# A hybrid encoder layer on one core: prompt attention with head pairs in TensorE row and column groups, expert gathers that skip empty places, gate and up weights in 8 KB pieces

## The reference

```python
h   = rmsnorm(x) * (1 + scale1) + shift1              # adaLN, modulation from silu(c) @ w_ada
q, k, v, cb, cc, cv, ga, gb = split(h @ w_in)         # 8 heads of 64
att = prompt_attention(q, k, v, rel_bias)             # per chunk of 64 frames: own + 8 previous chunks
                                                      # softmax(q k^T / 8 + bias(distance)) @ v
att_s = sample_attention(...)                         # 16 new frames against 512 cached keys + themselves
mix = (sigmoid(ga) * (att @ w_pa) + sigmoid(gb) * (short_conv(cb, cc, cv) @ w_pb)) @ w_o
x  += gate1 * mix
h2  = rmsnorm(x) * (1 + scale2) + shift2
# MoE: top-1 of 4 groups, then top-2 of its 8 experts; 32 experts, 1024 -> 512 -> 1024 (SwiGLU)
y   = sum over 2 experts of weight * (silu(h2 @ w_gate[e]) * (h2 @ w_up[e])) @ w_down[e]
x  += gate2 * y;  out = rmsnorm(x) * final_g
```

## Time and profile before

| | us |
|---|---|
| median of 3 runs | 1829.62 (1826.26 to 1830.77) |
| the profiled execution, its own time | 1827.22 |
| its span, first to last instruction | 1825.5 |
| PE busy | 1657.6 (91%) |
| DVE busy | 936.5 (51%) |
| ACT busy | 755.9 (41%) |
| POOL busy | 260.9 (14%) |
| mean granted TensorE clock | 0.959 of full |

### The profile page before, as it was taken

The page is one execution under the profiler, slowest core; times in us unless marked ns, Lnnn a source line. Parts: engine busy times, 40 slices in busy tenths (PEclk is TensorE's granted clock), DMA queues, the critical chain, the costliest instruction groups (busy, mean ns, idle before and its releaser), DMA issues.

```text
span 1825.5 us, 23013 instructions
## 1 busy us (share of the span) xinstructions
PE 1657.6 (91%) x8761; PEld 1380.1 (76%) x8761; DVE 936.5 (51%) x1108; ACT 755.9 (41%) x869; POOL 260.9 (14%) x327
## 2 busy tenths in 40 slices
PE   6994999999899999999998992499999999999977
PEld 1244997888599899999997882377787778777853
DVE  0450110555502552222224447488888888888857
ACT  0221221665311121112112222177777777777753
POOL 2003601110000000000000004112122121212003
PEclk9996999999999999999999996699999999999988
DMA  9857612000921111112126332399999999999967
GB/s 342 291 109 178 247 58 67 30 1 1 329 71 47 36 39 48 53 56 79 52 63 216 113 104 104 119 398 398 398 399 398 399 398 399 397 400 396 400 219 285
DMA packets 194748, 371.37 MB, mean 203 GB/s; under 512 B 10699, under 2 KB 69107, under 8 KB 194546
## 3 DMA queue, kind: packets, MB, share of 16 engines
q1 hardware_dynamic: 170784, 289.92, 43.9%
q0 software_dynamic: 18976, 62.93, 10.7%
q10 hardware_dynamic: 4914, 17.49, 2.4%
HBM read 324.49 MB, written 47.89 MB: 204 GB/s over the span
## 4 chain that ended last, share of the span: by engine, by line
PE 71%; DMA 13%; DVE 8%; issue 3%; ACT 3%; another core or an unknown queue 2%; SPq 0%; POOL 0%; DVEq 0%; ACTq 0%; PEldq 0%; POOLq 0%
PE ps L1547 13%; PE ps L1548 12%; PE ps L1549 12%; DMA mraw<-in_w_e_down_dram 10%; PE ps L1530 4%; PE ps L1876 4%; PE ps L1877 3%; PE ps L1883 3%; PE ps L1674 3%; PE ps L1655 2%; PE ps L1903 2%; PE ps L1911 2%; PE ps L1904 2%; ACT mhi L931 2%
## 5 line engine op out<-in xcount | busy, mean ns | idle before, releaser
L1064 DVE TENSOR_TENSOR mlo<-mraw,mhi 128x2048 fp32r<-128x2048 f32 x188 | 427.7, 2290 | 79.0 <-ACT mhi L931 78.8
L931 ACT CAST mhi<-mraw 128x2048 fp32r<-128x2048 f32 x192 | 366.8, 1914 | 113.5 <-DMA mraw<-in_w_e_down_dram 78.4
L1547 PE MATMUL ps<-hTh,ring_r 128*128 128x384 f32 x864 | 293.8, 340 | 34.6 <-DVE ring_r L1064 28.5
L1548 PE MATMUL ps<-hTl,ring_r 128*128 128x384 f32 x864 | 292.9, 339 | 0.0
L1549 PE MATMUL ps<-hTh,ring_r 128*128 128x384 f32 x864 | 292.6, 339 | 0.0
L1876 PE MATMUL ps<-mhi,xTh 128*128 128x512 f32 x512 | 204.7, 400 | 2.7 <-DVE xTl L1064 2.4
L1877 PE MATMUL ps<-mhi,xTl 128*128 128x512 f32 x512 | 201.3, 393 | 0.0
L1547 PEld LDWEIGHTS ps<-hTh,ring_r 128*128 128x128 f32 x864 | 165.5, 192 | 35.9 <-DVE ring_r L1064 26.7
L1064 DVE TENSOR_TENSOR ring_r<-ring_f,ring_r 128x1024 fp32r<-128x1024 f32 x56 | 68.3, 1224 | 198.5 <-ACT ring_r L741 198.1
L1549 PEld LDWEIGHTS ps<-hTh,ring_r 128*128 128x128 f32 x864 | 165.4, 191 | 0.0
L1548 PEld LDWEIGHTS ps<-hTl,ring_r 128*128 128x128 f32 x864 | 165.4, 191 | 0.0
(11 more groups left out here) (306 smaller groups left out, 2513.0 us busy)
## 6 DMA issues: line engine op xcount, KB each, us to landing
mraw<-in_w_e_gate_dram SPq DMA_DIRECT2D x64, 1024.0 KB
mraw<-in_w_e_up_dram SPq DMA_DIRECT2D x64, 1024.0 KB
mraw<-in_w_e_down_dram SPq DMA_DIRECT2D x64, 1024.0 KB, 12.6
aring<-in_w_ada_dram SPq DMA_DIRECT2D x24, 1024.0 KB
ring_f<-in_w_in_dram SPq DMA_DIRECT2D x80, 256.0 KB, 4.5
y_d<-yy ACTq DMA_DIRECT2D x32, 512.0 KB, 6.8
y_d<-zrow POOLq DMA_DIRECT2D x68, 128.0 KB, 4.0
kc<-in_cache_attn_k_dram SPq DMA_DIRECT2D x8, 1024.0 KB, 7.8
```

The lines of the kernel that those rows point to most:

```text
L931: nc.scalar.copy(mhi[j][:], mraw[j][:]).then_inc(s["gu_hi" if j < 4 else "d_hi"], 1)
L1064: V.tensor_tensor(out, value, high.bitcast(F32), ALU.subtract).then_inc(sig, 1)
L1547: mm(out, xh, wh, start=start, stop=False)
L1548: mm(out, xh, wl, start=False, stop=False)
```

## The change

Prompt attention: the scores of both heads of a pair are issued together, each with its own 64 partitions of `qT` and `kT` (row groups) and no `qz`. After the exponentials DVE computes the reciprocal of each unit's sum, and POOL multiplies the unit's probabilities by it in place. `S` gets four buffers, holds scores and probabilities, and `PT` gets three. The values of both heads are made together, `v` as the stationary operand with 64 columns, each head in its own column group, so the result comes out transposed as `qT` wants it; `att_t` and the multiplication on DVE go. PE order per pair p: scores(p+2), prob_t(2p), values(p-1), prob_t(2p+1).

Experts: empty places hold an index beyond the rows, and the gather skips these. The 1024 input features are numbered p*8+k instead of k*128+p for gate, up and router weights, so that a partition's four rows are one piece of 8 KB; h2 is written in that order by the DVE addition that makes it.

```diff
-        qz = at("qz", [P, 2, 2, P], A(148.25))
-        S = at("S", [P, 2, BAND], X(0))
-        Pr = at("Pr", [P, 2, BAND], X(5))
-        PT = at("PT", [P, 2, 5, P], X(10))
-        attt = at("attt", [P, 2, P], X(15))
+        S = at("S", [P, 4, BAND], X(0))
+        PT = [at(f"PT{j}", [P, 5, P], X(10 + 2.5 * j) if j < 2 else A(148.25)) for j in range(3)]
...
-            gate_d = w_e_gate[0].rearrange("e (k p) n -> p e k n", p=P)
-            up_d = w_e_up[0].rearrange("e (k p) n -> p e k n", p=P)
+            gate_d = w_e_gate[0].rearrange("e (p k) n -> p e k n", p=P)
+            up_d = w_e_up[0].rearrange("e (p k) n -> p e k n", p=P)
...
-            nc.gpsimd.memset(qz[:], 0.0).then_inc(s["zrow_ok"], 1)
-            pool.wait_ge(s["zrow_ok"], 2)
-            for pair in range(HP * NPT):
-                hp, i = pair // NPT, pair % NPT
-                wait(pool, s["s_scores"], 2 * pair - 2)
-                for h_ in range(2):
-                    rows = slice(HD * h_, HD * h_ + HD)
-                    nc.gpsimd.tensor_copy(qz[rows, pair % 2, h_, :], qT[rows, hp, i * P:(i + 1) * P]
-                                          ).then_inc(s["qz_ok"], 1)
+            for a in range(H * NPT):
+                c0 = P * (4 - min(a // 2 % NPT, 4))
+                pool.wait_ge(s["s_ri"], a + 1)
+                nc.gpsimd.tensor_scalar(S[:, a % 4, c0:BAND], S[:, a % 4, c0:BAND], rinv[:, a:a + 1], None,
+                                        ALU.mult).then_inc(s["s_n"], 1)
...
-                                        in_offset=bass.IndirectOffsetOnAxis(ap=idx[:, r:r + 1], axis=0)
+                                        in_offset=bass.IndirectOffsetOnAxis(ap=idx[:, r:r + 1], axis=0),
+                                        bounds_check=T - 1, oob_is_err=False
...
+            act.wait_ge(s["y_zeroed"], 16 * OVF * (D // 256))
             exp_rows(0)
-            for a in range(NA):
-                if a + 1 < NA:
-                    exp_rows(a + 1)
-                prob_cols(a)
+            exp_rows(1)
+            for p in range(NPAIR):
+                if p + 1 < NPAIR:
+                    exp_rows(2 * p + 2)
+                prob_cols(2 * p)
+                if p + 1 < NPAIR:
+                    exp_rows(2 * p + 3)
+                prob_cols(2 * p + 1)
...
-                dve.wait_ge(s["s_scores"], a + 1)
-                wait(dve, s["s_p"], a - 1)
+                dve.wait_ge(s["s_scores"], a // 2 + 1)
+                wait(dve, s["s_pt"], a - 3)
...
+            def normed(a):
+                dve.wait_ge(s["s_p"], a + 1)
+                V.reciprocal(rinv[:, a:a + 1], rowsum[:, a:a + 1]).then_inc(s["s_ri"], 1)
...
-                V.tensor_tensor(h2[:, r, :], h2[:, r, :], shift2[:, side, :], ALU.add).then_inc(s["n2_h"], 1)
+                V.tensor_tensor(h2[:, r, :].rearrange("t (k p) -> t p k", k=KT),
+                                h2n[:].rearrange("t (p k) -> t p k", k=KT),
+                                shift2[:, side, :].rearrange("t (p k) -> t p k", k=KT), ALU.add
+                                ).then_inc(s["n2_h"], 1)
...
-            V.tensor_copy(table[:], ps[:, 2, 0:NBLK]).then_inc(s["route_done"], 1)
+            link(V.tensor_scalar(blki[:], ps[:, 2, 0:NBLK], 0.0, EMPTY, ALU.is_equal, ALU.mult))
+            V.scalar_tensor_tensor(out=table[:], in0=ps[:, 2, 0:NBLK], scalar=-1.0, in1=blki[:],
+                                   op0=ALU.add, op1=ALU.add).then_inc(s["route_done"], 1)
...
+            def scores(p):
+                hp, i = p // NPT, p % NPT
                 j0 = 4 - min(i, 4)
-                pe.wait_ge(s["qz_ok"], 2 * (a // 2) + 2)
-                wait(pe, s["s_sb"], a - 1)
+                wait(pe, s["s_sb"], 2 * p)
                 k0 = (i - 4 + j0) * P
+                heads = [(2 * h_, slice(HD * h_, HD * h_ + HD)) for h_ in range(2)]
                 if j0 < 4:
-                    mm(bank(2 * (a % 2))[:, j0 * P:512], q, kT[:, hp, k0:i * P], start=True, stop=True)
+                    for b, rows in heads:
+                        mm(bank(b)[:, j0 * P:512], qT[rows, hp, i * P:(i + 1) * P], kT[rows, hp, k0:i * P],
+                           start=True, stop=True)
...
+            def values(p):
+                hp, i = p // NPT, p % NPT
+                pe.wait_ge(s["s_ptc"], 2 * p + 2)
+                wait(pe, s["s_attc"], p - 1)
                 j0 = 4 - min(i, 4)
                 for j in range(j0, 5):
-                    last = mm(ps[:, 6, HD * h_:HD * h_ + HD], PT[:, a % 2, j, :],
-                              v[:, i - 4 + j, (2 * hp + h_) * HD:(2 * hp + h_ + 1) * HD],
-                              start=(j == j0), stop=(j == 4))
+                    for h_ in range(2):
+                        last = mm(ps[HD * h_:HD * h_ + HD, 6 + p % 2, 0:P],
+                                  v[:, i - 4 + j, (2 * hp + h_) * HD:(2 * hp + h_ + 1) * HD],
+                                  PT[(2 * p + h_) % 3][:, j, :], start=(j == j0), stop=(j == 4))
```

More of the change, by code:

```diff
@@ L39 @@
 SEQROW = SEQS
+EMPTY = 65536.0
 TC = T // 3
@@ L1659, in prob_t @@
+                for b, rows in heads:
+                    last = mm(bank(b + 1)[:, 0:P], qT[rows, hp, i * P:(i + 1) * P], kT[rows, hp, i * P:(i + 1) * P],
+                              start=True, stop=True)
+                last.then_inc(s["s_scores"], 1)
             def prob_t(a):
[L1660 to L1661 removed]
+                i = a // 2 % NPT
+                pe.wait_ge(s["s_n"], a + 1)
                 wait(pe, s["s_ptc"], a)
                 for j in range(4 - min(i, 4), 5):
[L1664 removed]
+                    last = tr(bank(4, 2)[:, j * P:(j + 1) * P], S[:, a % 4, j * P:(j + 1) * P], ident[:])
@@ L1677, in values @@
                 last.then_inc(s["s_pv"], 1)
-            def att_t(pair):
-                pe.wait_ge(s["s_at"], pair + 1)
-                wait(pe, s["s_attc"], pair)
-                tr(ps[:, 7, 0:P], attt[:, pair % 2, :], ident[:]).then_inc(s["s_att"], 1)
             scores(0)
             scores(1)
-            for a in range(NA):
-                if a + 2 < NA:
-                    scores(a + 2)
-                prob_t(a)
-                if a >= 1:
-                    values(a - 1)
-                if a % 2 == 1 and a >= 3:
-                    att_t(a // 2 - 1)
@@ L1694, in _ @@
-            values(NA - 1)
-            att_t(NA // 2 - 1)
-            pe.wait_ge(s["s_attc"], HP * NPT)
+            for p in range(NPAIR):
+                if p + 2 < NPAIR:
+                    scores(p + 2)
+                prob_t(2 * p)
+                if p >= 1:
+                    values(p - 1)
+                prob_t(2 * p + 1)
+            values(NPAIR - 1)
+            pe.wait_ge(s["s_attc"], NPAIR)
             def old_keys_t(q, half):
```

97 lines of the change are left out of this document (38 added, 59 removed).

## The result

The changed kernel takes 1854.1 us (median of 4 runs, 1852.9 to 1855.5), the kernel before 1829.8 (4 runs, 1826.3 to 1830.8). The ratio is 1.0138, with a 95% interval from 1.0122 to 1.0154: slower by 1.4%. The forecast was 1803 and faster.

What follows compares the result with a forecast made beforehand. PE was taken to bound the prompt attention, transfers (PE nearly) the experts. Attention with start -12.6, experts -15 and small terms +0.6 gave -27.0: 1827.2 to 1800.2, plus 2.4 for the median, about 1803 us; range 1786 to 1828.

Steps and rivals of the forecast that it cites:

- The start: Before the first scores: PE no longer waits for POOL's first `qz`, gaining 3.0 us.
- The overlap of the heads: Prompt attention, five blocks: both heads overlap fully on PE, scores taking 1.08 us and values 1.1 (1.25 at the row's rate).
- The rivals in which the pairings fail: Attention heads do not overlap in scores or values: one failing ends at 1829 (chance 0.10), both at 1855 (0.03).
- POOL's multiplication: Attention, scaling 128x640 probabilities beside the scores: 0.95 us, between 0.68 (fill) and 1.41 (two inputs).
- the ring: Attention round of mask, scores beside POOL, transposes, values, transposes: 4.80 us for five blocks against 5.33; stage 131.4, 9.6 less.
- the clock: Rival: PE idles in the new attention ring and its clock falls to 1.2 GHz, +78 us, ending at 1881; chance 0.06.
- POOL slow: Rival: POOL multiplies at the two-input rate, attention gains almost nothing, ending at 1815; chance 0.05.
- The transposes: Attention on PE, five blocks: 2 x 0.54 = 1.08 us per round, as before.
- shape changes: Changes of PE array shape, three per attention round: 0.1 us each, 0.3 in all (0 to 0.45).
- The experts: Experts' stage: skipped rows and larger pieces speed transfers, PE binds next at 17.92 us per expert against 18.42; -15 us.
- ACT's wait for the down weights: Sign in the experts' stage: this wait, 73.7 us before, would be mostly gone.
- Small terms: Table's extra DVE instruction +0.2 us, strided h2 addition +0.4, router weights 0: +0.6 together.

Runs made afterwards that it cites:

- Kernel 2: Changed kernel with the probabilities scaled by DVE behind each reciprocal instead of by POOL: 1817.6 us.
- Kernels 6 and 7: Both on Kernel 2. First: six buffers of S, four of PT, 1806.6 us. Second: PE's scores behind the values, DVE's copy behind maxima and scalings, 1808.6 us.
- kernel 9: Changed kernel (POOL scaling) with six buffers of S, four of PT, and DVE's copy of the attention columns last in its round: 1799.1 us.
- kernel 10: As kernel 9, but scaling on DVE and gathers that fetch all 128 places (no skipping): 1788.1 us.
- kernel 8: Kernel before the change, plus only the 8 KB weight pieces and strided h2 addition; gathers fetch all rows: 1811.0 us.
- kernel 1: Kernel before the change, plus the experts' half alone (skipping gathers, 8 KB pieces, strided h2 addition); attention as before: 1816.3 us.
- kernel 11: Kernel before the change, plus only the skipping of empty places in gathers; gate and up pieces stay at 2 KB: 1826.7 us.

## Why the prediction was wrong, step by step

**The start.** -3.0 forecast, -2.7 measured. Right, as near as it can be told: it took 311.8 to 314.4 in the kernels with the new attention, 314.5 to 317.1 in those with the old one.

**The overlap of the heads.** Scores in 1.08 forecast: 0.97 for four blocks of both heads, 1.28 with the fifth. Values 1.1 to 1.25: 1.24. The rivals in which the pairings fail are refuted: twenty value instructions for two heads take 1.24, ten for one head and its result's transposition 1.18. The Trainium skill ("TensorE: Matmul & The Clock Gate", Part 3) has weight loads overlap running matmuls only where the row group differs. The trace doesn't agree with what the prediction drew from it, that the values of two heads would then not pair: they do, in the 1.24 above.

**POOL's multiplication: the step that failed.** I bounded it by a fill (0.68) and a two-input form (1.41), both scaled by columns, took 0.95, and let the upper one end the range. It is 1.88, 1.94 in the mean. The forms take 603, 923, 1243 and 1564 ns for 128 to 512 columns and 1.88 us for 640, so 2.5 ns per column and 0.28 us fixed, while the two-input subtraction, 2048 columns in 4.51, needs 2.2 per column. That a multiplication with one input can't be slower than a subtraction with two was an assumption, no row. With 1.94 in my own sum the round is 5.79, close to the 5.97 measured, and 1.0 more per full round is 24 us by the prediction's own scale: the 23 found above. This term alone turns the 1803 into 1827, still inside the stated range. The 1854 took the two terms below as well, the ring and the clock.

**The rival for it.** "POOL slow" was there with 0.05 and a price of 12 us, ending at 1815. The price was too small because of the assumed upper bound, and the chance most likely for the same reason; the case should have been worked out to where it turns the sign. The prediction gave 0.5 us of multiplication a price of 12, so its gain of 27 was gone at 0.95 + 1.1, about 2.1 us: twice the value taken, half above the bound.

**The rest of the ring.** Kernel 2 has no POOL in it and still takes 5.21, where my terms with 1.08 for the scores give 4.66. The transposes are the term that was furthest off: 0.70, and 0.91 until DVE starts, together 1.61, against 1.08 and part of the 0.30 for shape changes; the scores of the fifth block took 0.31, not 0.22, the values 1.24, which is the 1.25 of the row's own rate and not the 1.10 that I put into the sum. Five transposes took 0.54 ahead of work of the same shape and take 0.70 ahead of another shape. That is 0.16 at this change where I had 0.10. The Trainium skill ("TensorEngine Tiling (Array Packing)", Key Properties) says that a change of the tiling mode drains the engine; the trace agrees in kind. With DVE scaling the stage measured 144.9 where the sum had 131.4: so even with a fast multiplication the attention would have lost 4 us, not won 10. The ring itself, not only one duration in it, was forecast too short. Kernels 6 and 7 show that a ring of four buffers was what bounds that stage (129.2 and 135.4). That it was, and that the remedy lies in the buffers, was in my description and not among my rivals.

**The clock.** It had a chance of 0.06 as a cause of its own. It fell, to 0.88 on average, and cost 10 to 17 us, but as a follower: PE idled because of POOL. In kernels 2, 6, 9 and 10, where POOL is out of the ring or keeps up, it is 1.00 over 330 to 430. I treated the two rivals as separate cases, and they came together. 13.5 for the ring (144.9 against 131.4), 23 for POOL and 17 for the clock are the 53 us between the 131.4 of the prediction and the 184.4 of the trace.

**The experts.** -15 forecast and 15 measured, but the reason was wrong. With 8 KB pieces alone the transfers run at 414 GB/s and PE is the bound at 17.72, without the 0.3 to 0.5 us of idle time that I left in. With both edits they run at 393 to 398, at a share of 1.00 to 1.01, where I expected less than 1.0. ACT's wait for the down weights did not go away, it grew from 73.7 to 97.3 in the same stage of the changed kernel (1220 to 1780 us there):

```profile
ACT mhi L933 <- DMA mraw<-in_w_e_down_dram: 97.3, 59, 3.2
```

In kernel 8 it is nearly as large, 87.0 over 1190 to 1740, while PE has hardly any idle time: so there it is the slack of an engine that runs ahead. What the path lost was PE's wait for `hh`, 8.4 us in 27 times. In kernel 8 it is 3.3 us, 3.0 of them once, at the start of the stage:

```profile
PE ps L1929 <- DVE hh L1450: 3.3, 2, 3.0
```

The number came out by luck, because two errors cancel. PE's own pace is 17.72, 0.20 better than the 17.92 that I took, and skipping, which I had at 0.55 in the transfers' favour, takes 0.18 back.

Why skipping costs 0.2 us per expert when the pieces are large is half open. The ten kernels with both edits took 17.90 to 17.97 per expert, the two without skipping 17.68 and 17.72, so the effect is there. Where the time goes, the waits over 1220 to 1700 us show: PE's weight loads for the hidden transposes wait for `hh` again, first with skipping (kernel 1), then without (kernel 8):

```profile
PEld ps L1934 <- DVE hh L1455: 7.1, 19, 0.7
PEld ps L1929 <- DVE hh L1450: 1.1, 2, 0.8
```

The 6.0 us between them are 0.22 per expert. Why `hh` comes later is not shown. The bytes fall by 0.23 MB per expert, the rate from 414 to 393 to 398 GB/s, more than the bytes do. Packets under 512 bytes rise from 3697 to 5350 over 1190 to 1700 us, 58 per expert, about as many as the 56 skipped rows. Whether the rows that remain sit on a few of the DMA engines, which would leave the slowest as late as before, these traces don't tell.

**Small terms.** The h2 addition with its strided output takes 2.01 us instead of 1.23 (nine of them), under other work; the stretch from the attention to the experts is 0.1 us longer. Forecast was +0.6, and the difference is too small to tell.

## What to carry to other kernels

When a change puts an instruction between two engines that feed each other through a few buffers, write the round as a ring with all its instructions, each engine's both halves, and ask for every wait which buffer or which place in an engine's order closes it. A slow engine at a side of the ring costs its latency until the ring is opened, and its rate after that: here the same multiplication cost 40 us with the clock that followed it, or 8 (kernel 9 against kernel 10). And an instruction that waits (here a 0.3 us copy) delays all that is queued behind it, so look whether it can stand last in its engine's round. It pays only where no other ring is longer: 32 us with six buffers, 3 at most with four.

## What the runs showed of the hardware

- GpSimd's multiplication of S by a value per partition, in place: 0.60 us for 128 columns, 1.88 for 640, where DVE takes 0.29 and 0.55 for the same.
- A multiplication of 640 columns that began within about 0.1 us of a DVE weight conversion (1.21 us, two inputs) took 2.84 (two of 32 in the changed kernel). In kernel 9, where POOL's multiplication had already run for 0.56 and 0.70 us when a conversion began, it took no longer than usual.
- Score matmuls of two heads in different row groups and value matmuls in different column groups both overlap; four blocks of two heads take 0.97 us, against 0.86 for one head before.
- TensorE's granted clock averaged 0.88 where PE was busy 108 of 160 us (changed kernel), and 1.00 where it was busy 73.8 of 100, with waits of 1.2 us there too (kernel 2). Within the changed kernel two full rounds with the same waits (1.22 and 0.70) had 1.00 and 0.77.
- Weight pieces of 8 KB per partition raised the transfer rate of the experts' stage from 399 to 414 GB/s (kernel 8); gathers that left out 56 of 128 rows lowered the bytes and the rate together, 399 to 389 with small pieces (kernel 11).
